# The first layer's recurrence set 6 units later in the order of work that it shares with the convolution branch's projection

## The chip, the cores and the metric

The kernel runs on one core of a Trainium2 chip. The metric is the device time in microseconds (us) of one execution; smaller is better. The engines of the core are TensorE (PE in the profile, with PEld for its weight loads), VectorE (DVE), ScalarE (ACT), GpSimd (POOL) and SyncE (SP, which issues the transfers). Each runs its own list of instructions in order and meets the others only at semaphores.

## The reference

The program is a stack of three layers over 512 tokens of width 1024 (with 256 context tokens in the first two), in fp32. What the change touches is the token mixer of the first layer. Its input projection feeds two halves: a gated linear recurrence over chunks in both directions (HGRN2), and a "chunk MLP" (the gelu branch, called the convolution branch in the change's short title; it is u and v below).

```python
def hgrn2_mixer(pl, pc, lb, onorm_w, with_ctx):
    ...
    oc_f, sc_f = gla_chunked(*fwd_c, s0)
    ol_f, _ = gla_chunked(*fwd_l, sc_f)
    oc_b, sc_b = gla_chunked(*[flip_t(a) for a in bwd_c], s0)
    ol_b, _ = gla_chunked(*[flip_t(a) for a in bwd_l], sc_b)

def chunk_mlp(u_pre, v_pre, vnorm_w, ws, bs):
    u = jax.nn.gelu(u_pre)
    v = rms_norm(jax.nn.gelu(v_pre).reshape(bsz, n, B_CHUNK, B_GROUPS, B_GROUP_DIM), vnorm_w)
    sv = jnp.einsum('gts,bnsgc->bntgc', ws, v) + bs.T[:, :, None]
    return u * sv.reshape(bsz, t_len, B_WIDTH)
```

In the recurrence each chunk of 128 tokens scores its own tokens against one another under a decay, reads the state that earlier chunks left, and updates it. A chunk therefore can't finish before the one ahead of it in its direction.

## The kernel before, in words

All that the change touches lies in one stage, `recurrence_and_mix` (L1565). Four programs share the engines in it:

- `flow`, a `Flow` (L215): the projection to v (4 tiles) and u (4 tiles) of the chunk MLP. A tile is 128 output rows by 768 tokens, summed over 8 slices, each three fp32 matmuls (high by high, high by low, low by high part), in two banks of 512 and 256 tokens (`parts=2`). On TensorE (L463) it is cut into slots of 6 matmuls, 8 to a tile. When a tile is done ScalarE runs the gelu on it (L1462; a load of the gelu table before it, and a load of the log-and-exp table behind it, L52) and then writes the high part `w_hi` of a later weight tile (L339). GpSimd then subtracts to get the low part `w_lo` (L380). VectorE multiplies u by the mixed v at the end (`gate`, L1472).
- `flow_g`: 4 more tiles of the same kind, for the recurrence's output gate (silu, L1595), right behind `flow`.
- `gl`, a `Recurrence` (L1114): 12 steps, one direction each in turn (6 chunks, 2 directions). Step n has on VectorE `keys` (L1209), `sums` (scans, L1218), `base_and_ends` (L1239, L1244), `levels` (L1228, L1229), `decayed_base` (L1256, L1257), `decayed` (L1267 to L1270), `merge` (L1289, L1292), `both` (L1300) and `update` (L1310). On ScalarE it has `log` (L1322), `grow_base` (L1330 to L1332), `grow` (L1338, L1339), `keys_back` (L1344) and `take` (L1350). On TensorE it has `turn_keys` (L1386), `scores` in two halves (L1397), `base_scores` (L1417), `read_out` (L1369, L1370) and `gain` (L1377). The stages of one step are staggered: `keys` of step n+3 stands beside `merge` of step n.
- `cm`, a `ChunkMix` (L1423): for each of the 4 tiles of v a chain between ScalarE, TensorE and VectorE: `Square` (L1486), a matmul with ones that sums (L1522), `Ln` (L1492), `Exp` (L1497), the norm (L1559), and for each of two halves a transpose (L1536), a copy (L1502), the mixing matmuls (L1544, L1547) and a copy out (L1506).

Some places hold matmuls on an identity that nothing reads (`keep_busy`, L57): 18 ahead of the first `scores`, 10 ahead of the first `turn_keys`, and 12, 6, 0 and 4 ahead of the norm of each v tile. Each fp32 matmul is two in the trace.

The four programs are generators, and `weave` (L87) takes the next piece of the program that the common list `order` names. The list is made by merging times in arbitrary units (`merged`, L81). One list serves ScalarE, VectorE and TensorE, so on each of them the instructions have one fixed order, which these times decide; the times themselves do nothing else. SyncE and GpSimd have no such list. The flows take one tile in 196/13 = 15.08 units. The recurrence's times come from `times(begin, pre, step)`: three opening slots of `pre` units, and then one slot of `step` units for each of the 12 steps, each cut in 8 turns:

```python
        order = merged(flow_times, even(flow_g.slots, flow.n * tile, (flow.n + flow_g.n + 1) * tile),
                       gl.times(0, 8, 14.3), mix_times)
```

`mix_times` hang on the flow's tiles and not on the recurrence.

Of the kernel before, what the change touches and what calls it, by code (L numbers as in the profile page):

```python
# [75 lines left out]
def even(n, a, b):  # L76

    return [a + (k + 0.5) * (b - a) / n for k in range(n)]


def merged(*times):  # L81

    turns = [(at, t) for t, own in enumerate(times) for at in own]
    return [t for _, t in sorted(turns)]


def weave(order, *programs):  # L87

    for t in order:
        next(programs[t], None)  # L90
    for program_ in programs:
        for _ in program_:
            pass
# [1471 lines left out]
def recurrence_and_mix(K, A, h_hi, h_lo, q, v, z, y_mlp, weights, x, g, nxt):  # L1565

    nc = K.nc
    with ExitStack() as c:
        W = A_HEADS * CHUNK
        rest = c.enter_context(nc.sbuf_tensor("ev_rest", [P, 17, W], F32))  # L1570
        rows = x[:, :, :].rearrange("p a t -> p (a t)").rearrange("p (r w) -> p r w", w=W)
        free = {"x": rows, "rest": rest[:, :, :]}
        at = {"x": 0, "rest": 0}

        def taken(name, n, work):
            where = "x" if name in ("k0", "k1", "S0", "S1", "kt", "ws", "gb", "sq") else "rest"
            a = at[where]
            at[where] += n
            return free[where][:, a:a + n, :]
        masks = K.rstd[:, :].rearrange("p (d t) -> p d t", d=2)  # L1580
        gl = Recurrence(K, c, q, v, z, masks, A["gla_masks"].rearrange("p (d t) -> p d t", d=2), None, taken)
        cm = ChunkMix(K, c, A["ws_t"], A["bs"], weights, y_mlp, None, taken)
        acc = [c.enter_context(nc.psum_tensor(f"uv_acc{j}", [P, 512], F32)) for j in range(3)]
        flow = Flow(K, c, "uv", A["ev_uv"], 2 * B_GROUPS, DT, h_hi, h_lo, 0, TOK,
                    [(1, cm.gelus)], [(2, cm.gate)],
                    (A["ev_g"], DT), acc=acc, parts=2, low_on_pool=True)
        space = [(cm.mixed, 2 * B_GROUPS), (cm.normed, B_GROUPS), (cm.gated, B_GROUPS - 1), (cm.gated, B_GROUPS)]

        def gates(act, f, i):
            act.wait_ge(*space[i])  # L1590
            for part in range(2):
                m = 2 * i + part
                act.wait_ge(f.mm_done, m + 1)
                at, _, width = f.banks[part]
                f.took(nc.scalar.activation(g[i][:, at:at + width], f.out(m)[:, 0:width], ACT.Silu), m)  # L1595
            K.log_and_exp()
        flow_g = Flow(K, c, "evg", A["ev_g"], A_HEADS, DT, h_hi, h_lo, 0, TOK, [(1, gates)], [], nxt, acc=acc, parts=2,
                      after=flow, then=2, low_on_pool=True)
        tile = 196 / (2 * B_GROUPS + A_HEADS + 1)
        flow_times = even(flow.slots, 0, (flow.n + 1) * tile)  # L1600
        mix_times = []
        for m in range(B_GROUPS):
            done = flow_times[(m + 1) * DT - 1]
            mix_times += even(cm.TURNS, done + 3.2, done + 3.2 + tile)
        mix_times.append(mix_times[-1] + 1)
        order = merged(flow_times, even(flow_g.slots, flow.n * tile, (flow.n + flow_g.n + 1) * tile),
                       gl.times(0, 8, 14.3), mix_times)
        with K.block() as block:
            @block.sync
            def _(sp):  # L1610
                gl.sp(sp)
                cm.sp(sp)
                weave([], flow.sp(sp))
                weave([], flow_g.sp(sp))

            @block.gpsimd
            def _(pool):
                flow.pool(pool)
                flow_g.pool(pool)

            @block.scalar
            def _(act):
                weave(order, flow.act(act), flow_g.act(act), gl.act(act), cm.act(act, flow))

            @block.vector
            def _(dve):
                weave(order, flow.dve(dve), flow_g.dve(dve), gl.dve(dve), cm.dve(dve))

            @block.tensor
            def _(pe):  # L1630
                weave(order, flow.pe(pe), flow_g.pe(pe), gl.pe(pe), cm.pe(pe))
# [2340 lines left out]
```

## Time and profile before

| | us |
|---|---|
| median of 3 runs | 2647.91 (2647.44 to 2651.93) |
| the profiled execution | 2654.73, span 2653.0 |
| TensorE busy in the span | 2522.3 (95%) |
| VectorE busy | 1669.1 (63%) |
| ScalarE busy | 988.7 (37%) |
| GpSimd busy | 172.9 (7%) |
| mean granted clock of TensorE | 0.986 |

Busy time is a sum over very different stages. The stage of this change is about a tenth of the span, from the first L463 matmul at 185.66 us to the last `update` at 438.72 us; what stands ahead of it and behind it is other code. Times in the trace are microseconds from the start of the span. TensorE's matmuls overlap, so the time that a group of them takes is best read as the distance between the starts of neighbouring groups.

### The profile page before, as it was taken

The numbers are of one execution on the slowest core, as the hardware profiler recorded it, in microseconds if no ns is written. First come the engines' busy times: TensorE is split into PE (matmuls) and PEld (weight loads), VectorE is DVE, ScalarE is ACT, GpSimd is POOL, SyncE is SP. The second block draws the span as 40 slices with busy tenths as digits, with TensorE's granted clock in tenths as the row PEclk, the third lists the DMA queues.
The fourth block names the chain that finished last, engine by engine and source line by source line (L and its number), as shares of the span: only waits on it lengthen the run. The fifth ranks groups of instructions, "written<-read, shape, count | busy, mean of one in ns | idle before, by whom it ended". The sixth has DMA issues, their size and how long they took to land. (4 is left out here: it accounts for less than half of the span.)

```text
span 2653.0 us, 36362 instructions
## 1 busy us (share of the span) xinstructions
PE 2522.3 (95%) x14741; PEld 2128.3 (80%) x14741; DVE 1669.1 (63%) x2706; ACT 988.7 (37%) x1362; POOL 172.9 (7%) x183
## 2 busy tenths in 40 slices
PE   8999899999999999999999999999989998989997
PEld 3888787788888888866679989977778886867786
DVE  5887697566767776444446756737967775354744
ACT  4235555332212222345443323325542224345532
POOL 0111011000000000012000000001610000000000
PEclk9999999999999999999999999999999999999998
DMA  6650012223343333221023443322210001211232
GB/s 261 197 160 18 23 33 88 72 87 96 101 154 119 97 104 108 70 71 48 1 72 120 137 149 125 116 82 76 80 58 17 17 9 48 96 60 68 80 103 80
DMA packets 62425, 232.26 MB, mean 88 GB/s; under 512 B 6961, under 2 KB 9649, under 8 KB 61618
## 3 DMA queue, kind: packets, MB, share of 16 engines
q1 hardware_dynamic: 46962, 173.82, 19.9%
q0 software_dynamic: 15296, 56.11, 6.7%
q8 instruction: 117, 1.92, 0.3%
q14 instruction: 50, 0.41, 0.1%
HBM read 227.02 MB, written 2.10 MB: 86 GB/s over the span
## 5 line engine op out<-in xcount | busy, mean ns | idle before, releaser
L395 DVE TENSOR_TENSOR w_lo<-w_raw,w_hi 128x1024 fp32r<-128x1024 f32 (+2 forms) x253 | 323.0, 1277 | 322.9 <-ACT w_hi L339 318.7
L339 ACT ACTIVATE w_hi<-w_raw 128x1024 fp32r<-128x1024 f32 (+4 forms) x284 | 298.1, 1050 | 253.8 <-PE late_acc L485 93.3
L485 PE MATMUL mid_acc<-mid_h_hi,w_hi 128*128 128x258 f32 x832 | 279.4, 336 | 1.5 <-DVE mid_od_fq L653 1.0
L485 PE MATMUL mid_acc<-mid_h_hi,w_lo 128*128 128x258 f32 x832 | 279.0, 335 | 0.0
L485 PE MATMUL mid_acc<-mid_h_lo,w_hi 128*128 128x258 f32 x832 | 277.1, 333 | 0.0
L485 PE MATMUL late_acc<-late_h_hi,w_hi 128*128 128x258 f32 x704 | 199.3, 283 | 0.0
L485 PE MATMUL late_acc<-late_h_hi,w_lo 128*128 128x258 f32 x704 | 198.4, 282 | 0.0
L485 PE MATMUL late_acc<-late_h_lo,w_hi 128*128 128x258 f32 x704 | 197.7, 281 | 0.0
L485 PEld LDWEIGHTS mid_acc<-mid_h_hi,w_hi 128*128 128x128 f32 x832 | 157.3, 189 | 19.4 <-issue 2.4
L485 PEld LDWEIGHTS mid_acc<-mid_h_lo,w_hi 128*128 128x128 f32 x832 | 157.5, 189 | 18.6 <-issue 1.2
L485 PEld LDWEIGHTS mid_acc<-mid_h_hi,w_lo 128*128 128x128 f32 x832 | 156.8, 189 | 16.1
L485 PE MATMUL mid_acc<-mid_y_hi,w_hi 128*128 128x256 f32 (+1 forms) x384 | 132.3, 344 | 5.8 <-DVE w_lo L395 5.2
L485 PEld LDWEIGHTS late_acc<-late_h_lo,w_hi 128*128 128x128 f32 x704 | 133.6, 190 | 0.5 <-issue 0.5
L485 PEld LDWEIGHTS late_acc<-late_h_hi,w_hi 128*128 128x128 f32 x704 | 133.1, 189 | 0.5 <-issue 0.5
L485 PEld LDWEIGHTS late_acc<-late_h_hi,w_lo 128*128 128x128 f32 x704 | 132.7, 188 | 0.0
L485 PE MATMUL mid_acc<-mid_y_lo,w_hi 128*128 128x256 f32 (+1 forms) x384 | 130.4, 340 | 0.0
L485 PE MATMUL mid_acc<-mid_y_hi,w_lo 128*128 128x256 f32 (+1 forms) x384 | 130.0, 338 | 0.0
L131 DVE CUSTOM_DVE_ANT_0 mid_scratch<-mid_side_raw,mid_rows 128x1024 f32<-128x1024 f32 x96 | 117.4, 1223 | 1.7
L3030 ACT ACTIVATE dr_low<-dr_bank 128x512 f32<-128x512 f32 x48 | 28.7, 597 | 177.5 <-PE dr_bank L3157 177.5
L485 PE MATMUL dq_acc<-s_h_hi,w_hi 128*128 128x512 f32 x200 | 85.7, 429 | 5.6 <-DVE s_h_lo L2612 4.2
L485 PE MATMUL qvz_acc<-ev_h_hi,w_hi 128*128 128x256 f32 (+1 forms) x256 | 87.1, 340 | 0.0
L485 PE MATMUL qvz_acc<-ev_h_lo,w_hi 128*128 128x256 f32 (+1 forms) x256 | 86.9, 339 | 0.0
(527 smaller groups left out, 6169.8 us busy)
## 6 DMA issues: line engine op xcount, KB each, us to landing
w_raw<-in_up SPq DMA_DIRECT2D x88, 512.0 KB, 3.6
mid_side_raw<-in_ada_t POOLq DMA_DIRECT2D x48, 512.0 KB, 3.8
w_raw<-in_down SPq DMA_DIRECT2D x32, 704.0 KB, 4.1
qvz_side_raw<-in_ada_t POOLq DMA_DIRECT2D x32, 512.0 KB, 4.3
w_raw<-in_dn_qkv SPq DMA_DIRECT2D x25, 512.0 KB, 3.2
late_side_raw<-in_ada_t POOLq DMA_DIRECT2D x24, 512.0 KB, 4.1
w_raw<-in_da SPq DMA_DIRECT2D x18, 512.0 KB, 3.2
w_raw<-in_ev_qvz SPq DMA_DIRECT2D x16, 512.0 KB, 4.3
```

Of the source, the lines that this page charges most:

```text
L131: nc.vector.tensor_tensor_reduce(out=self.scratch, in0=self.raw[:, j, :], in1=self.rows[:, m, :], scale=1.0, scalar=0.0, op0=ALU.mult, op1 ...
L339: nc.scalar.activation(K.whi[:, g % 2, 0:width], K.raw[:, g % 2, 0:width], ACT.Copy).then_inc(K.hi_done, 1)
L395: nc.vector.tensor_tensor(K.wlo[:, g % 2, 0:width], K.raw[:, g % 2, 0:width], K.whi[:, g % 2, 0:width].bitcast(F32), ALU.subtract).then_in ...
L485: last = nc.tensor.matmul(self.acc[i % len(self.acc)][:, at:at + width], left[:, j, cols], right[k][:, moving:moving + width], start=((i, ...
L3030: nc.scalar.activation(XL[G][:, :], bank[G][0][:, :], ACT.Copy).then_inc(A[G].empty, 1)
```

## The change

The recurrence's times begin at 6 units instead of 0. All of its pieces keep their order among themselves, and so do the pieces of the flows and of the chunk MLP. What changes on ScalarE, VectorE and TensorE is how the two lists are interleaved: each piece of the recurrence now stands behind the pieces of the others whose time is up to 6 units later than its old one (6/14.3 = 0.42 of a step, 6/15.08 = 0.40 of a tile). No instruction is added or removed.

```diff
         order = merged(flow_times, even(flow_g.slots, flow.n * tile, (flow.n + flow_g.n + 1) * tile),
-                       gl.times(0, 8, 14.3), mix_times)
+                       gl.times(6, 8, 14.3), mix_times)
```

Written out from the list, the order on ScalarE around the first two tiles is (numbers are the step or tile, with the half behind the point):

```
before: log0 log1 grow_base0 grow0 gelu0 w_hi square0 ln0.0 log2 ln0.1 keys_back0 exp0 grow_base1 grow1 copy0.0
        out0.0 copy0.1 take0 log3 gelu1 w_hi out0.1 square1 ln1.0
after:  log0 gelu0 w_hi square0 log1 ln0.0 ln0.1 grow_base0 grow0 exp0 log2 copy0.0 keys_back0 out0.0 copy0.1
        grow_base1 grow1 gelu1 w_hi out0.1 square1 ln1.0
```

and the end of TensorE's, with g3 as the last tile of `flow_g` (a slot each):

```
before: read_out10 g3 gain10 g3 g3 turn_keys11 scores11.0 g3 scores11.1 g3 base_scores11 read_out11 gain11
after:  read_out10 g3 gain10 g3 turn_keys11 scores11.0 scores11.1 base_scores11 read_out11 gain11
```

## Rows read from the trace of the kernel before

**Rows 1.** Stretches: width; busy (count) of PE, PEld, DVE, ACT, POOL; clock, DMA, GB/s

```profile
185.60:304.50 118.90, 106.63 (x697) 92.64 (x698) 81.71 (x182) 63.84 (x89) 12.58 (x5) 0.94 0.11 33
304.50:425.50 121.00, 115.39 (x814) 106.24 (x813) 107.10 (x255) 71.24 (x90) 16.99 (x7) 0.99 0.09 27
425.50:438.80 13.30, 10.50 (x89) 9.92 (x87) 6.00 (x16) 5.20 (x6) 2.35 (x1) 1.00 0.00 1
```

**Rows 2.** TensorE in order of time, opening: start, us, what, [idle before]

```profile
204.72 1.65 PE L1522 MATMUL cm_ps<-x,ones 128*128 128x384 f32 x2 [7.73 <-ACT x L1486]
...
211.71 4.18 PE L57 MATMUL gl_bank<-ident 128*128 128x128 f32 x36
...
223.66 2.84 PE L57 MATMUL cm_ps<-ident 128*128 128x128 f32 x24
```

**Rows 3.** TensorE in order of time, from transpose 1.1 to the sum of square 2

```profile
254.46 0.55 PE L1536 MATMUL cm_ps<-ident,x 128*128 128x128 f32 x3
254.84 1.06 PE L1377 MATMUL gl_bank<-ev_v,x 128*128 128x128 f32 x8
255.65 0.47 PE L463 MATMUL uv_acc<-ev_h_hi,w_hi 128*128 128x512 f32 x1
...
257.21 0.91 PE L1544 MATMUL cm_ps<-ev_rest,ones 1*128 1x384 f32 x2
...
258.74 0.47 PE L463 MATMUL uv_acc<-ev_h_hi,w_hi 128*128 128x512 f32 x1
...
260.20 0.60 PE L1386 MATMUL gl_bank<-ident,ev_rest 128*128 128x128 f32 x4
260.64 1.90 PE L1397 MATMUL gl_bank<-ev_rest 128*128 128x64 f32 x16
262.37 0.86 PE L1522 MATMUL cm_ps<-x,ones 128*128 128x384 f32 x2
```

**Rows 4.** ScalarE's groups, 183 to 445 us: count, busy us, mean ns, idle before

```profile
L1339 ACT ACTIVATE ev_rest<-ev_rest 128x2560 f32<-128x2560 f32 x12 | 27.9, 2327 | 0.0
...
L339 ACT ACTIVATE w_hi<-w_raw 128x1024 fp32r<-128x1024 f32 x13 | 13.8, 1059 | 3.7 <-PE uv_acc L463 2.0 <-PEq L1085 1.7
L1462 ACT ACT_TABLE_LOAD x8 | 10.3, 1283 | 0.1
...
L1462 ACT ACTIVATE x<-uv_acc 128x512 f32<-128x512 f32 (+1 forms) x16 | 7.0, 488 | 0.1
...
L1486 ACT ACTIVATE x<-x 128x768 f32<-128x768 f32 x4 | 3.3, 832 | 0.0
```

**Rows 5.** Waits, 183 to 445 us: total, times, longest

```profile
PE cm_ps L1536 <- DVE x L1559: 4.5, 2, 2.7
```

**Rows 6.** VectorE in order of time, single lines of the stage

```profile
204.37 2.84 DVE L1244 TENSOR_TENSOR ev_rest<-ev_z 128x512 f32<-128x512 f32 x1
...
304.47 0.43 DVE L1209 TENSOR_SCALAR x<-ev_z 128x512 f32<-128x512 f32 x1
...
332.38 1.98 DVE L1289 COPY_PREDICATED x<-rstd,gl_bank 128x256 f32<-128x256 uint32 x4
...
362.19 3.47 DVE L1218 TENSOR_TENSOR_SCAN ev_z<-ones,ev_z 128x128 f32<-128x128 f32 x4
...
402.06 2.12 DVE L1256 TENSOR_TENSOR ev_rest<-x,ev_rest 128x512 f32<-128x512 f32 x1
...
421.59 0.43 DVE L1267 TENSOR_TENSOR ev_rest<-ev_q,ev_rest 128x256 f32<-128x256 f32 x1 [2.73 <-ACT ev_rest L1339]
```

**Rows 7.** GpSimd in order of time, low parts of weight tiles

```profile
204.01 2.65 POOL L380 TENSOR_TENSOR w_lo<-w_raw,w_hi 128x1024 fp32r<-128x1024 f32 x1 [14.84 <-ACT w_hi L339]
...
332.43 2.40 POOL L380 TENSOR_TENSOR w_lo<-w_raw,w_hi 128x1024 fp32r<-128x1024 f32 x1 [13.57 <-ACT w_hi L339]
...
362.83 2.54 POOL L380 TENSOR_TENSOR w_lo<-w_raw,w_hi 128x1024 fp32r<-128x1024 f32 x1 [12.00 <-ACT w_hi L339]
...
401.21 2.42 POOL L380 TENSOR_TENSOR w_lo<-w_raw,w_hi 128x1024 fp32r<-128x1024 f32 x1 [14.83 <-ACT w_hi L339]
```

## What the change does to the time: a prediction

> **What bounds the kernel now.** I read the stretches of the stage first, then the waits, then each engine in order of time. The stage has three parts. In the opening, 118.9 us up to `keys6`, TensorE is busy 106.6 us and VectorE only 81.7, and the granted clock is 0.94 in the mean: about (1 - 0.94) x 118.9 = 7.1 us of clock is missing, that is some 14 us at 1.2 GHz instead of 2.4 [rows 1]. Here the four chains of the chunk MLP run between the projection's slots, and TensorE is the engine that the others wait for. From `keys6` at 304.47 us [rows 6] to the end of `decayed11` VectorE is busy 107.1 of 121.0 us and TensorE 115.4, but TensorE's matmuls overlap and its busy time flatters it [rows 1]. The steps come about every 16 us, and a step's VectorE work is about 14.5 us, to which a `gate` of 0.95 comes in four of them, so VectorE sets the beat. In the tail of 13.3 us only the last step's chain is left [rows 1].
>
> Two single facts matter. TensorE stands 7.73 us ahead of the first sum of squares, since ScalarE does `grow0`, the gelu, a `w_hi` and two table loads before the square; when it starts, the two matmuls take 1.65 us where they take 0.86 later [rows 2, 3]. And the 36 filler matmuls at 211.71 and 24 at 223.66, 4.0 and 2.7 us, cover no wait here: what they stand in front of was ready [rows 2].
>
> **Part 1, the opening: what goes.** In the new order `gelu0`, `w_hi` and `square0` stand ahead of `log1`, `grow_base0` and `grow0` on ScalarE. The gelu can start when the first tile is done at about 194.3. From there table load 1.28, `w_hi` 1.06, square 0.83 [rows 4], with 0.4 for the gelu's second half: the sum can start at about 197.9 instead of 204.7. TensorE has come to it at 196.9, so 7.7 us of waiting become 1.1, and 2.3 us of slow clock behind it go. The two waits of transposes on the norm (4.5 us together, [rows 5]) and the slow clock after the longer (about 1.7) go too, since the norm is not late there in the new order, and about 2 us of small gaps. Together 18 us go.
>
> **Part 1: what comes.** First, the norm of tile 0 now stands behind `decayed0` on VectorE, which waits for `grow0`, which waits for `ln0.1`. I walked this: sum 0.0 at 197.9, two slots, sum 0.1 to 202.2, `ln` 0.5, `grow_base0` 1.25, `grow0` 2.9 to 206.9, `decayed0` 4.0, `keys2` 0.4, norm 1.0: 212.3. TensorE has done two slots and the 24 fillers by 206.2, and waits 6.1 us; about 1.9 us of slow clock follow, by the 10 us at the low level that the 7.73 us wait brought. Second, at tiles 1, 2 and 3 ScalarE has `grow`, gelu, `w_hi`, copy out and square in a row behind the transposed half's copy: 0.5 + 2.85 + 2.2 + 2.25 + 0.5 + 0.75 = 9.05 us (2.33 of it L1339, 2 x 1.28 the tables, [rows 4]). TensorE has in that time, between transpose and next sum, a slot 1.46, mixing 1.53, a slot 1.46, and in two cases `read_out` 1.75: 4.5 to 6.2 us, so it waits 2.9 to 4.6 us each time. Before, `grow` was out of this row (6.2 us) and TensorE had 262.37 - 254.84 = 7.5 us of work in the same place, with `gain`, `turn_keys` and half the scores [rows 3], and waited for nothing. My walk gives waits of 4.9, 2.8 and 3.5 us, with 1.2 at one mixing: 12.4 us, and 1.3 of slow clock after the first. Sum of what comes: 1.1 + 6.1 + 1.9 + 12.4 + 1.3 = 22.8 us, beyond 18 less small gaps that come back (1.5): about 6 us more at equal TensorE work. Slow clock after the waits of 2.8 and 3.5 us would add up to 3; I carry 1. For the recurrence it is more, since its pieces are also 0.42 of a step later: the walk has `decayed4` end at 314.5, where it ended at 304.5. **Opening: +10.0 us** at `keys6`, with 5 and 14 as bounds (the three waits at zero for the lower, and all of them with slow clock for the upper).
>
> **Part 2, the steps in rhythm.** The same VectorE work, but two of its losses change. VectorE stood 121.0 - 107.1 = 13.9 us [rows 1], 2.73 of it at `decayed11`, behind a silu and `w_hi` that stand between `grow_base11` and `grow11` [rows 6]; in the new order they never stand there, and with VectorE busier the small waits for `gain` and `base_scores` shrink. I keep 2.9 us of idle time.
>
> Against that, the low parts on GpSimd move. Where one of them overlaps a VectorE instruction that reads two tensors from SBUF, or a scan, VectorE stands until it is over: L1244 took 2.84 us at 204.37, beside the low part at 204.01; the scans took 3.47 at 362.19 instead of 1.37, beside 362.83; L1256 took 2.12 at 402.06 instead of 0.69, beside 401.21 [rows 6, 7]. Where it overlapped four merges out of PSUM, at 332.43, they took 1.98 us, as always [rows 6, 7]. Before, the low parts of this part hit for 2.1 + 1.4 + 0.4 = 3.9 us; three of them fell on merges. In the new order a tile's last slot stands behind `base_scores` and not ahead of `turn_keys`, so gelu or silu, `w_hi` and low part come some 5 to 7 us later in the step: from 12 us after an `update`, when VectorE is in `decayed` (to 12.9), `keys`, or the next `base_and_ends` (from 14.9). Seven low parts, walked one by one: 2.1, 2.1, 2.1, 2.1, 1.2, 1.7, 1.6 = 12.9 us. So the part takes 107.1 - 3.9 + 12.9 + 2.9 = 119.0 us instead of 121.0: **-2.0 us**. With only 4 us of hits the part would be 9 us shorter than I say, at -11; with 2.1 at all seven and 8 us of idle time left it would be 125.9 us, at +5.
>
> The Trainium skill states this in the GPSIMD Engine Reference, sections Specifications and Key points: GpSimd shares its SBUF interfaces with VectorE, and they contend when a VectorE instruction has two SBUF inputs or runs in a two-port mode. It speaks against the change, and by that rule, the trace agrees: 2.84 us beside GpSimd, 0.69 alone. Taken as a full block of 2.4 us each, the seven would cost 16.8 us and not 12.9; the sum above stays with the rows.
>
> **Part 3, the tail.** The last two slots of the gate projection stood between the halves of `scores11` and ahead of `base_scores11`; now all slots are done. From the end of `decayed11`: `both10` and `update10` 1.8, `turn_keys` 0.43, scores 1.73 twice, base 0.9, last merge 0.75, `read_out` 1.8, `gain` 0.8, `update11` 1.15: 11.1 us instead of 13.3. **-2.1 us**. The slots themselves cost nothing elsewhere, since they lie in waits of TensorE for VectorE. The silu and the weight split that also stood there are done earlier or lie beside this chain. Transfers: the weight loads are released by `w_hi` and low parts and land in about 4 us, with two tiles of lead; they move by less than a tile and cost nothing.
>
> **Sum.** 10.0 - 2.0 - 2.1 = +5.9 us, and 1 for slow clock in the opening: +7 us. The profiled execution took 2654.73 us, 6.8 above the median of 2647.91; I take the shift as the same for both: 2661.7 for a profiled one, 2654.9 for the median. **2655 us.**
>
> **Rivals.**
> - *Faster: the first wait decides.* The 7.73 us and its clock are gone, and the waits at sums 1 to 3 don't arise, because `grow` ends earlier than I have it (each 2.9 us of `grow` must then be done before the transpose). The opening is then some 14 us shorter than I say, at -4, and with -2.0 and -2.1 the stage ends 8 us earlier: 2640. It decides where the three waits sum to less than about 3 us. Against it: `grow_base` and `grow` stand behind the copies in ScalarE's own order, so they can't run ahead.
> - *About the same: the low parts mostly miss.* If they fall on `both`, `update` and merges, which read PSUM, at most 4 us of the 12.9 are left: +7 - 9 = -2 us, 2646. A shift of 2 us in either engine does this, and my walk is no finer than that.
> - *Slower still.* All seven hits in full (+2), idle time of VectorE that stays at 8 us (+5): 2662.
> - That the change does nothing is out: the lists differ at nearly every entry.
>
> **How the numbers follow.** The forecast, 2650 to 2660, has 0.5; the faster rival 0.12; the low parts missing 0.22; slower still 0.16. What a measurement can tell from no change is about 0.2%, 5.3 us: below 2642.6 faster, above 2653.2 slower. Of the forecast's 0.5 I put 0.34 above that line and 0.16 within it; of the faster rival all but 0.01 below, of the missing low parts 0.02 below. Faster 0.13, same 0.37, slower 0.50. The range of 2643 to 2665 leaves out most of the faster rival and the far end of the slower one.
>
> **What would show it.** Right: TensorE's wait ahead of the first sum falls from 7.7 us to 1 or 2; a new wait of about 6 us ahead of the fillers' transpose (L1536 on the norm L1559); waits of 3 to 5 us on L1486 at the three later sums; `keys6` about 10 us later; VectorE's L1267, L1209 or L1239 with single instructions of 2 to 2.5 us; the last `update` about 11 us behind `decayed11`, where it was 13.3. Wrong: no waits on L1486 behind the first, or low parts that all lie beside merges.

## The result, and the profile after

| | before | after |
|---|---|---|
| median of five executions, us | 2650.00 (2647.44 to 2651.93) | 2673.49 (2662.23 to 2679.56) |
| ratio after / before | | 1.0073, 95% interval [1.0052, 1.0094] |
| profiled execution, us (span) | 2654.73 (2653.0) | 2662.83 (2661.1) |
| the stage, first L463 matmul to the next stage's first VectorE operation, us | 185.66 to 439.05 | to 451.57 |

The change makes the kernel slower by 0.73% (19 us; the medians lie 23.5 us apart); the forecast was 7 us, and 2673.49 lies above its range. A second series of the same kernel (`e1_again`, below) gave 1.0052 [1.0038, 1.0066], 14 us, with 11.4 us between the medians. Both are slower, and neither is 7 us. One execution of `e1_again` (5054.56 us) and one of `e3_late_split` (3629.84 us) stand far outside all others and are left out of the medians and ratios below.

The five executions of after differ more than those of before: two took 2662.2 and 2662.8 us at a mean granted clock of 0.987 and 0.986, three took 2673.5 to 2679.6 at 0.983 to 0.980. Between the first and the last lie 17.3 us; the missing clock is (1 - 0.987) x 2660.5 = 35 us in the one and (1 - 0.980) x 2677.8 = 54 us in the other, 19 us more. The missing clock is an upper bound of its cost, since clock that is missing while TensorE waits costs nothing, but it is of the size of the whole spread. The profiled execution is one of the two that lost least.

The stretches of the stage in after, divided as in [rows 1] (at `keys6`, the end of `decayed11` and the last `update`); columns are width, busy time (count) of PE, PEld, DVE, ACT and POOL, granted clock, DMA share, GB/s:

```profile
185.60:316.20 130.60, 111.80 (x715) 96.25 (x716) 76.65 (x181) 65.55 (x92) 11.85 (x5) 0.95 0.09 30
316.20:439.50 123.30, 115.25 (x807) 105.75 (x806) 116.39 (x255) 70.56 (x89) 19.18 (x7) 0.97 0.09 27
439.50:451.30 11.80, 9.12 (x78) 8.54 (x76) 5.88 (x15) 3.21 (x4) 2.36 (x1) 1.00 0.00 1
```

Against [rows 1] the opening is 11.7 us longer. TensorE is idle for 18.8 us of it, where it was for 12.3, and its busy column grows by 5.2 us, part of which is work at the low clock. The rhythm part is 2.3 us longer, with VectorE busy 116.39 us where it was 107.10. The tail is 1.5 us shorter.

TensorE in order of time in after, the instructions that had stood for over 0.8 us on ScalarE or VectorE in the opening, and one at `turn_keys5`: start, us, what, [idle before]:

```profile
197.67 0.91 PE L1522 MATMUL cm_ps<-x,ones 128*128 128x384 f32 x2 [0.83 <-ACT x L1486]
212.15 0.90 PE L1536 MATMUL cm_ps<-ident,x 128*128 128x128 f32 x3 [6.05 <-DVE x L1559]
238.88 1.65 PE L1522 MATMUL cm_ps<-x,ones 128*128 128x384 f32 x2 [4.95 <-ACT x L1486]
268.84 0.91 PE L1522 MATMUL cm_ps<-x,ones 128*128 128x384 f32 x2 [2.70 <-ACT x L1486]
293.73 0.91 PE L1522 MATMUL cm_ps<-x,ones 128*128 128x384 f32 x2 [3.09 <-ACT x L1486]
312.60 0.91 PE L1544 MATMUL cm_ps<-ev_rest,ones 1*128 1x384 f32 x2 [1.18 <-ACT x L1502]
339.27 0.70 PE L1386 MATMUL gl_bank<-ident,ev_rest 128*128 128x128 f32 x4 [3.50 <-DVE ev_rest L1310]
```

The 7.73 us wait of [rows 2] is gone and a row of new ones stands behind it. The second and the third take 0.90 and 1.65 us for what takes 0.55 in [rows 3] and 0.91 in the rows below: they run at 1.2 GHz. The clock around the two long waits in after (columns as above):

```profile
203.20:210.00 6.80, 2.90 (x26) 2.71 (x25) 4.57 (x11) 4.13 (x5) 0.00 (x0) 1.00 0.00 0
210.00:216.80 6.80, 4.65 (x22) 4.66 (x23) 6.76 (x17) 1.12 (x2) 0.00 (x0) 0.50 0.00 0
...
237.40:244.20 6.80, 5.32 (x20) 4.62 (x21) 0.24 (x1) 2.01 (x4) 2.35 (x1) 0.50 0.25 77
```

The clock halves (0.50 of 2.4 GHz) from 210.0 and from 237.4, each time within the wait and on for 4.6 and 5.3 us of the work behind it. VectorE's instructions from `keys6` on that took far longer than others of their line (x4: four scans together):

```profile
319.68 2.79 DVE L1239 TENSOR_TENSOR ev_rest<-ev_z 128x512 f32<-128x512 f32 x1
...
334.84 2.47 DVE L1209 TENSOR_SCALAR x<-ev_z 128x512 f32<-128x512 f32 x1
...
355.58 2.50 DVE L1209 TENSOR_SCALAR x<-ev_z 128x512 f32<-128x512 f32 x1
...
369.94 2.57 DVE L1267 TENSOR_TENSOR ev_rest<-x,ev_rest 128x256 f32<-128x256 f32 x1
...
395.64 3.52 DVE L1218 TENSOR_TENSOR_SCAN ev_z<-ones,ev_z 128x128 f32<-128x128 f32 x4
...
412.80 3.50 DVE L1218 TENSOR_TENSOR_SCAN ev_z<-ones,ev_z 128x128 f32<-128x128 f32 x4
...
425.59 1.98 DVE L1239 TENSOR_TENSOR ev_rest<-ev_z 128x512 f32<-128x512 f32 x1
```

and beside them GpSimd's low parts:

```profile
319.54 2.39 POOL L380 TENSOR_TENSOR w_lo<-w_raw,w_hi 128x1024 fp32r<-128x1024 f32 x1 [24.54 <-ACT w_hi L339]
333.29 3.74 POOL L380 TENSOR_TENSOR w_lo<-w_raw,w_hi 128x1024 fp32r<-128x1024 f32 x1 [11.36 <-ACT w_hi L339]
354.73 3.07 POOL L380 TENSOR_TENSOR w_lo<-w_raw,w_hi 128x1024 fp32r<-128x1024 f32 x1 [17.70 <-ACT w_hi L339]
369.79 2.45 POOL L380 TENSOR_TENSOR w_lo<-w_raw,w_hi 128x1024 fp32r<-128x1024 f32 x1 [11.98 <-ACT w_hi L339]
396.11 2.46 POOL L380 TENSOR_TENSOR w_lo<-w_raw,w_hi 128x1024 fp32r<-128x1024 f32 x1 [23.87 <-ACT w_hi L339]
412.67 2.72 POOL L380 TENSOR_TENSOR w_lo<-w_raw,w_hi 128x1024 fp32r<-128x1024 f32 x1 [14.11 <-ACT w_hi L339]
424.67 2.35 POOL L380 TENSOR_TENSOR w_lo<-w_raw,w_hi 128x1024 fp32r<-128x1024 f32 x1 [9.28 <-ACT w_hi L339]
```

All seven that fall in the part stop VectorE. Less the usual 0.69, 0.43, 0.43, 0.42, 1.37, 1.37 and 0.69 us of the same work, the seven take 13.9 us too much. The Trainium skill says in the GPSIMD Engine Reference, section Key points, that GpSimd's SBUF interfaces are VectorE's too, for instructions with two SBUF inputs or in a two-port mode; the trace agrees for those with two inputs. L1209 reads a single tensor and stood all the same; by that page it would be of the second kind, but no run here shows in which mode it runs.

The first two stops have a sequel: they make the `update` behind them late, `turn_keys5` waits for that (3.50 us above), the clock halves from 339.8 to 346.6, the scores are late, and VectorE stands in its turn:

```profile
348.08 0.90 DVE L1289 COPY_PREDICATED x<-rstd,gl_bank 128x256 f32<-128x256 uint32 x2 [2.88 <-PE gl_bank L1397]
```

In `e17_after_cut` below, the same order with these low parts cut short, that wait of `turn_keys5` (L1388 there) falls to 0.15 us:

```profile
338.17 0.66 PE L1388 MATMUL gl_bank<-ident,ev_rest 128*128 128x128 f32 x4 [0.15 <-DVE ev_rest L1312]
```

### The profile page after: what moved, and what is told of

Same layout as the page of the kernel before. It is cut to its first block and busy times, and to the rows that moved or that the text cites. A ratio compares the mean times of both kernels' runs of the same rounds, so it can differ in the third digit from the quotient of the medians.

```text
span 2661.1 us, 36361 instructions
## 1 busy us (share of the span) xinstructions
PE 2521.9 (95%) x14741; PEld 2127.7 (80%) x14741; DVE 1673.1 (63%) x2706; ACT 987.7 (37%) x1361; POOL 174.4 (7%) x183
```

## The experiments

The questions. Theory A, from the prediction and the trace of after: the loss has three parts, the new order itself (waits at full clock), the clock that halves in the waits, and VectorE beside GpSimd. Rivals: the loss is the opening alone; or the steps alone; or something behind the stage. The experiments divide the change in place (`e4`, `e5`, `e6`), move the low parts (`e3`, `e7`), hold the clock by filling waits (`e2`, `e12`, `e13`) and take the low parts away (`e9`, `e10`, `e14` to `e18`). Each ratio is to the kernel before, run in the same series on the same chip. Diffs are against the kernel after, unless said otherwise.

**The change again**, with nothing edited.

> The changed kernel once more, to see where the executions differ from the profiled one. The profiled execution took 2662.8 us, 12.9 us over the median of the kernel before, which is what a walk through the orders gives for this stage (+10 in the opening, -2, -2); but three of five executions took 2673.5 to 2679.6 us with a mean granted clock of 0.980 to 0.983 instead of 0.986. Theory A (clock): the new short waits of TensorE in the opening (6.05, 4.95, 3.09, 2.70 us) are followed by the low clock in some executions and not in others. Then the longer executions are longer inside the stage from 185 to 451 us, by low clock that the trace shows there. Theory B (elsewhere): the stage takes 265 us in all executions, and the rest of the kernel runs at a lower clock in some. The median is expected at 2668 to 2678 by both; if a trace of a longer execution comes, the place of the low clock tells them apart.

Median 2665.76 against 2654.33: 1.0052 [1.0038, 1.0066]; its executions lie between 2662.5 and 2674.3 us, and their mean is 13.7 us above that of before. Its profiled execution took 2674.32 us, and its stage ends at 459.1, 7.5 us behind that of the other profile. It is the same kernel, with the same waits (6.04, 4.95, 2.72 and 3.09 us in the opening); what differs is the clock. Its stretches at 1.2 GHz up to 356 us (columns as above):

```profile
211.80:218.60 6.80, 5.94 (x28) 5.94 (x29) 5.97 (x15) 1.03 (x2) 0.00 (x0) 0.50 0.00 0
...
239.10:245.90 6.80, 5.88 (x21) 5.09 (x22) 0.00 (x0) 1.44 (x3) 2.17 (x1) 0.50 0.27 77
269.90:273.30 3.40, 3.02 (x6) 2.12 (x7) 0.00 (x0) 0.91 (x2) 1.64 (x1) 0.50 0.25 33
297.20:300.60 3.40, 3.40 (x13) 2.86 (x12) 1.20 (x5) 1.10 (x2) 0.64 (x1) 0.50 0.49 142
345.00:355.20 10.20, 10.20 (x44) 9.62 (x43) 5.50 (x16) 5.90 (x8) 0.00 (x0) 0.50 0.00 0
```

Here all four long waits halve the clock, where in the first profile two did. The stage spends 34 us at 1.2 GHz, against 20.5 in the first profile of after and 17.1 in before.

**The waits filled.** Filler matmuls go where the four long waits of the opening were, so that TensorE works through them. Another 12 were meant for the wait at `turn_keys5`.

> The changed kernel with matmuls on the identity, which nothing reads, put into TensorE's waits: 34 instead of 12 ahead of the norm of tile 0 (wait of 6.05 us), 18, 9 and 10 ahead of the sums of squares 1, 2 and 3 (4.95, 2.70, 3.09 us), 12 ahead of turn_keys 5 (3.50 us). The waits themselves stay, so nothing but the granted clock can change. Theory A (clock decides the spread and some 11 us of the median): no fall of the clock in the stage, the spread of the executions shrinks to 5 us, and the median comes to 2654 to 2660 (the profiled 2662.8 less 3 to 8 us of low clock). Theory B (the clock falls elsewhere): median and spread stay within 3 us of the changed kernel's. Theory C (the order alone costs what the median shows): the clock in the stage is 1.0 and the median stays at 2670 or more.

```diff
-    BUSY_KEYS = {0: 10}
+    BUSY_KEYS = {0: 10, 5: 12}
...
+                    if g:
+                        pe.wait_ge(self.gl.merged, 5 * g)
+                        K.keep_busy(self.gl.ps_s[0][:, 0:P], (0, 18, 9, 10)[g])   # ahead of sum g
...
-                    K.keep_busy(self.ps[:, 0:P], (12, 6, 0, 4)[g])
+                    K.keep_busy(self.ps[:, 0:P], (34, 6, 0, 4)[g])                # ahead of the transpose
```

Median 2662.16, 1.0032 [1.0021, 1.0043], executions 2657.9 to 2666.0. The waits in the opening shrink to 1.13, 0.94, 0.71 and 0.88 us, `keys6` starts at 311.3 (316.2 and 320.7 without), and 4 us between the medians, 5.5 between the means, are gone. No work of the kernel was moved, and the wait for a merge that the edit adds shows no idle time in the trace, so these were clock. They are less than filling the opening is worth, because the fillers of `turn_keys5` missed their wait: in `turn_keys` the wait for the `update` stands ahead of `keep_busy`, so they came behind it and were work more, some 4.3 us up to L1386:

```profile
334.36 4.44 PE L57 MATMUL gl_bank<-ident 128*128 128x128 f32 x24 [3.49 <-DVE ev_rest L1310]
338.63 0.60 PE L1386 MATMUL gl_bank<-ident,ev_rest 128*128 128x128 f32 x4
```

Against the first profile of after, `keys6` is 4.9 us earlier and the stage ends (450.9) only 0.7 us earlier. `e12`, `e13`, `e14` and `e11` below have such fillers too (4.4, 2.6, 1.9 and 2.1 us in their traces); `e15` and `e18` don't. The opening of `e2` and the rest of the stage (columns as above):

```profile
185.60:311.30 125.70, 120.02 (x833) 105.22 (x832) 76.62 (x181) 65.28 (x92) 11.81 (x5) 1.00 0.10 31
311.30:450.60 139.30, 128.59 (x906) 118.49 (x904) 122.39 (x269) 73.73 (x92) 21.52 (x8) 0.96 0.08 24
```

**Only the short waits filled**: as above, but none at the transpose (12 as in the kernel) nor at sum 1.

> The changed kernel with fillers in its shorter waits only: 9 and 10 ahead of the sums of squares 2 and 3 (2.7 and 3.1 us) and 12 ahead of turn_keys 5 (3.5 us); the waits of 6.05 us ahead of the norm's transpose and 4.95 us ahead of the first sum stay bare. The clock fell behind the two long waits in every trace of this kernel, but behind the sums 2 and 3 only in the longer execution. Theory A says that the short ones make the spread and the gap between the profiled execution and the median: then executions within 5 us of one another, median 2660 to 2665 with low clock only behind the two long waits. If the long ones decide: 2666 or more.

Median 2668.87, 1.0065 [1.0051, 1.0079]: nothing gained at the end. Its clock halves at 209.8 and 237.1, in the waits of 6.05 and 5.00 us, and no longer in the short ones; `keys6` comes at 316.1, as in the first profile of after and 4.6 us ahead of `e1_again`. Behind that it has the 4.4 us of misplaced fillers. So the run shows that the two long waits bring the slow clock by themselves, but not that the short ones cost nothing.

**Low parts later in the step.** The split of a weight tile is issued at a later turn.

> The changed kernel with the high part of each weight tile of both projections (ScalarE), and with it the low part (GpSimd), four turns later in the tile, so that the low parts fall beside the merges again and no longer beside VectorE's instructions with two SBUF inputs. Theory D (the seven or so hits of 1.2 to 2.1 us are paid by the end, about 13 us in all against 4 before): VectorE has no instruction of over 2 us in the steps in rhythm, and the time is 6 to 10 us below that of the changed kernel. Theory E (TensorE bounds the steps as well, VectorE's stalls are hidden): the long instructions vanish and the time falls by less than 3 us. In the opening the square no longer stands behind the high part (2.25 us less in front of each sum), which by the walk takes up to 2 us from each of the waits at sums 1 to 3: 3 to 6 us more.

```diff
-                    (A["ev_g"], DT), acc=acc, parts=2, low_on_pool=True)
+                    (A["ev_g"], DT), acc=acc, parts=2, low_on_pool=True, split_turn=5)
...
-                      after=flow, then=2, low_on_pool=True)
+                      after=flow, then=2, low_on_pool=True, split_turn=5)
```

Median 2662.84, 1.0032 [1.0020, 1.0044]. Three to five us better than `e1_again`, but this didn't take the stalls away: behind `keys6` they moved to scans (323.5, 340.9, 358.3) and to L1257 and L1256 (364.9, 428.5), and four came into the opening, where the one at 207.7 goes with a wait on the norm of 8.19 us instead of 6.05. `e7_late_split7`, the same with 7 in place of 5:

> The changed kernel with the high and low parts six turns later in the tile instead of four, since with four they fell on the scans just ahead of the merges (VectorE's long instructions were still worth 10 us in the steps in rhythm, of 14). With six they should fall on the merges, which read PSUM. Theory D (the stalls of VectorE beside GpSimd are paid by the end): at most two instructions of over 2 us in the steps in rhythm, the stretch from keys 6 to the last update takes 125 to 128 us instead of 135, and the time is 8 to 12 us below that of the changed kernel. Theory E (they are hidden): the stretch stays at 131 or more.

Median 2666.04, 1.0054 [1.0042, 1.0067]. Behind `keys6` low parts again hit a scan (319.7) and L1256, L1257 and L1267 (341.3 to 428.9). Neither run isolates the stalls. With VectorE busy nine tenths of the time, a low part of 2.4 us finds nearly no place.

**The change by halves.** Only the three opening slots of the recurrence's times are later, and closer together, so that its steps begin at 24 units as before (`e4`); or only the steps are 6 units later (`e5`); or all is 3 units later in place of 6 (`e6`).

> The recurrence begins at 6 units, but its three opening slots are 6 units wide instead of 8: 6 + 3 x 6 = 24, so its twelve steps stand where they stand in the kernel before, and only the start is late. Theory F (the first wait of 7.7 us is won, the losses come from the steps' place): 4 to 8 us faster than the kernel before, no waits on the later squares, low parts beside the merges as before. Theory G (the late start itself costs: the norm of tile 0 waits for decayed of step 0): the first wait is gone but one of 3 to 6 us ahead of the norm's transpose stands in its place, and the time is within 4 us of the kernel before.

```diff
-                       gl.times(6, 8, 14.3), mix_times)
+                       gl.times(6, 6, 14.3), mix_times)
```

> The complement of the last experiment's opening: the recurrence's three opening slots stand where they stand in the kernel before (0 to 24 units), and only its twelve steps are 6 units later, as in the changed kernel. Theory F (the losses come from the steps' place, the opening's shift is a gain of about 9 us): TensorE's first wait is 7.7 us again, the waits on the squares 1 to 3 (5, 3, 3 us) and the low parts beside VectorE's own work are there, and the time is 20 to 30 us above the kernel before, that is 8 to 12 us above the changed kernel. Theory G (the late opening is what costs in the changed kernel): the time is within 5 us of the kernel before.

```diff
-                       gl.times(6, 8, 14.3), mix_times)
+                       [t if t < 24 else t + 6 for t in gl.times(0, 8, 14.3)], mix_times)
```

> Half the change: the recurrence begins at 3 units instead of 6. Its first grow_base and grow then stand at 19.5 and 20.5 units, still behind the first gelu (17.9) and square (18.0), so the first wait of 7.7 us goes here as well; grow of steps 1, 2 and 3 stands at 29.7, 44.0 and 58.3 units, ahead of the second halves' copies at 30.5, 45.6 and 60.7 and 3 to 5 units ahead of the gelus. Theory H (what costs is grow directly ahead of gelu, high part and square on ScalarE): no waits of over 2 us at the squares 1 to 3, and the time is 3 to 10 us below the kernel before. Theory I (the cost grows with the shift): it is between the two, at 5 to 9 us above the kernel before.

```diff
-                       gl.times(6, 8, 14.3), mix_times)
+                       gl.times(3, 8, 14.3), mix_times)
```

| kernel | median, us (before beside it) | ratio | `keys6` | end of the stage |
|---|---|---|---|---|
| `e4_opening_only` | 2645.01 (2654.33) | 0.9963 [0.9950, 0.9975] | 295.2 | 429.8 |
| `e5_steps_only` | 2671.68 (2652.64) | 1.0075 [1.0061, 1.0088] | 321.1 | 460.0 |
| `e6_begin3` | 2651.97 (2652.64) | 0.9997 [0.9988, 1.0006] | 297.1 | 436.7 |
| before, profiled | | | 304.5 | 439.05 |

The change is the sum of two opposite ones. Its opening slots alone, with the gelu of tile 0 ahead of `grow0`, are worth 9 us: the first wait falls to 1.10 us, the one on the norm of tile 0 doesn't come up, and the opening runs at full clock throughout (columns as above):

```profile
185.60:295.20 109.60, 103.04 (x697) 89.33 (x698) 81.83 (x181) 62.43 (x88) 12.32 (x5) 1.00 0.11 36
```

The steps alone cost 19 us, and have waits of 7.23, 5.84, 2.71 and 3.12 us with 44 us at 1.2 GHz. The sum of the two, 10 us, is near the change's 11 to 14 in the second series. `e4` beats both kernels. With 3 units the three waits at the sums aren't there: the point at which `grow` comes into ScalarE's row ahead of the square lies between 3 and 6. In `e6` the wait of an L463 on a gelu is 5.04 us (at 356.61; 1.75 in before), and the low parts hit scans; its total is that of before.

**Fewer fillers.** In `e4` the fillers stand in front of work that is ready, as in [rows 2]. `e8_opening_trim` leaves most of them out, `e11_trim_held` puts 9 at `turn_keys5` besides (`BUSY_KEYS = {0: 0, 5: 9}`). Against `e4`:

> The order that was 9 us faster than the kernel before (opening at 6 with slots of 6 units), with fewer matmuls that nothing reads: none instead of 10 ahead of the first turn_keys, 10 instead of 18 ahead of the first scores, 6 instead of 12 ahead of the norm of tile 0. In that kernel's trace they stood in front of work that was ready, and a wait of 2.3 us for decayed of step 0 is left to cover. Expected by those rows: 4 to 5.5 us below the opening alone, about 2640. If the granted clock falls in the opening for want of them, the gain is lost: 2645 or more, with low clock between 200 and 230 us.

```diff
-    BUSY_KEYS = {0: 10}
+    BUSY_KEYS = {0: 0}
...
-                self.K.keep_busy(self.ps_s[0][:, 0:P], 18)
+                self.K.keep_busy(self.ps_s[0][:, 0:P], 10)
...
-                    K.keep_busy(self.ps[:, 0:P], (12, 6, 0, 4)[g])
+                    K.keep_busy(self.ps[:, 0:P], (6, 6, 0, 4)[g])
```

> The shifted opening with trimmed fillers, whose opening was 3 us shorter than without the trimming (keys 6 at 292.1 us instead of 295.2) but whose last update ended at the same time: its trace shows 10.2 us at the low clock from 315.5 us, behind a wait of 2.31 us ahead of turn_keys 5, where the untrimmed one has 3.4 us. This kernel has 9 matmuls on the identity (2.0 us) in that wait. Theory A (short waits are paid through the clock): no low clock between 310 and 340 us, the last update some 3 us earlier (at about 426.5 instead of 429.5), the time 2640 to 2643. Rival: the steps in rhythm are bound by VectorE and absorb the 3 us whatever the clock: last update at 429.5 and 2644 to 2646.

Medians 2644.68, 0.9972 [0.9961, 0.9983], and 2645.15, 0.9973 [0.9962, 0.9983]: no better than `e4`. In `e8` `keys6` comes 3.1 us earlier than in `e4`, and the stage ends at the same 429.8, with 10.2 us at 1.2 GHz from 315.5 (3.4 us in `e4`); in `e11` the low stretch is at 217.1 (6.8 us) instead, and `keys6` is back at 295.3. The expectation of `e11` failed. It didn't test what it was meant to, since its 9 fillers came behind the wait at `turn_keys5` (2.33 us). Why the clock falls at 217.1, where TensorE was busy throughout, stays open; the wait ahead of that, 1.69 us, is in `e8` as well (1.68), and there the clock stays up.

**Without the low parts.** To price the stalls, GpSimd computes 128 of the 1024 columns of each low part, so seven eighths of the low parts are left out of the computation.

```diff
-            nc.gpsimd.tensor_tensor(K.wlo[:, g % 2, 0:width], K.raw[:, g % 2, 0:width],
-                                    K.whi[:, g % 2, 0:width].bitcast(F32), ALU.subtract).then_inc(K.lo_done, 1)
+            nc.gpsimd.tensor_tensor(K.wlo[:, g % 2, 0:P], K.raw[:, g % 2, 0:P],
+                                    K.whi[:, g % 2, 0:P].bitcast(F32), ALU.subtract).then_inc(K.lo_done, 1)
```

The order of before with this is `e9_before_short_low`, with its waits filled too `e14_before_filled_short_low`; the order of after is `e10_after_short_low` and, with the fillers of `e2` in the opening alone, `e15_after_filled_short_low`. `e13_before_filled` is before with its waits filled alone (30 ahead of the first sum, 10 and 10 at the norms; `BUSY_KEYS = {0: 10, 5: 8}`, which again comes behind its wait).

> The kernel before with GpSimd's low parts in this stage cut to the first 128 of each row's 1024 columns (the other seven eighths of the low part are left out, so the projection's result lacks that correction): each takes about 0.35 us instead of 2.4 and can stall VectorE for no more than that. It is the partner of the next run. Before, VectorE's long instructions beside GpSimd are worth about 10 us in the whole stage (2.1 us at 204, 238, 261 and 362, 1.4 at 402, 0.4 at 386), most of them where TensorE or ScalarE is what the stage waits for. Theory D (stalls are paid by the end): 3 to 5 us below the kernel before. Theory E (hidden): within 2 us of it.

> The changed kernel with the same cut of the low parts. In its trace the stalls are worth 14 us in the steps in rhythm alone. Theory D: it is 10 to 16 us faster than the changed kernel (2668), so 3 us below to 5 above the kernel before, and the stretch from keys 6 to the last update takes 122 to 126 us instead of 135. Theory E: it is less than 5 us faster than the changed kernel.

> The kernel before with fillers in its own waits: 30 ahead of the first sum of squares (7.7 us), 10 instead of 0 and 4 ahead of the norms' transposes of tiles 2 and 3 (2.7 and 1.7 us), 8 ahead of turn_keys 5 (2.3 us). Partner of the changed kernel with its waits filled (2662, 6 us below the unfilled). Its low clock in the opening is 13.7 us, of which some 8 lie beside work. Theory J (each order loses by the clock, the changed one some 6 us and the old one about 4): 2647 to 2650. Theory K (only the changed order loses by the clock): 2651 or more.

> The kernel before with both taken away, VectorE's stalls beside GpSimd (low parts cut to an eighth) and the bare waits (filled). By the single runs: stalls -9.1, clock -2 to -5 if theory J holds; the sum is 2638 to 2641. It is the baseline of the next run: what is left between the two is the order alone, by waits of one engine for another.

> The changed kernel with both taken away: its stalls were worth 17 us (2668 to 2651) and its bare waits 6 (2668 to 2662). If the two are independent: 2645, with keys 6 at 312 us and 127 us from there to the end of the stage. Then the order alone is worth 4 to 6 us beside the partner run, stalls 8 and clock 2 to 4 of the 15 us that the change costs. If filling no longer helps once the stalls are gone (2650 or more), the clock mattered only through them.

This cut also reached three projections of the second layer whose low parts GpSimd computes, so only differences between these kernels hold, not their distance to before. The last three restrict it to the flows of this stage (`if self.name in ("uv", "evg"): width = P` ahead of the same line).

> The kernel before, with GpSimd's low parts of this stage's flows alone computed on 128 of 1024 columns (seven eighths of these low parts are left out; the second layer's keep their whole width). Theory A (about 8 to 9 us of the change's price is VectorE and GpSimd standing beside each other, 8.0 us of such stalls in the old order with its waits filled): the stage's own share here is 2 to 5 us below before, about 2648 to 2650, and the second layer's share of the earlier cut was 5 to 7 us. Rival B (the second layer had no share): 2643 again.

> The changed kernel with the same cut of this stage's low parts alone. Theory A: 10 to 12 us below the changed kernel, 2656 to 2658, which is 6 to 8 us above the kernel before with the same cut. Rival B: 2651 again.

> The changed kernel with its four long waits filled (as in e2_filled) and this stage's low parts cut. Theory A (order alone +2 to 3, clock 5 to 6, stalls about 9): 2650 to 2653, that is 4 to 7 us below e17_after_cut and 1 to 4 us above e16_before_cut. Rival B (the sizes came from the second layer's low parts): no nearer to e16_before_cut than e2_filled is to the kernel before, 8 us above it.

Medians as distance to the kernel before of the same series, us, with the ratio:

| | low parts whole | cut everywhere | cut in the stage alone |
|---|---|---|---|
| order of before | 0 | `e9` -9.1, 0.9965 [0.9952, 0.9977] | `e16` -1.8, 0.9993 [0.9984, 1.0002] |
| the same, filled | `e13` -1.0, 0.9995 [0.9986, 1.0003] | `e14` -9.0, 0.9961 [0.9948, 0.9973] | |
| order of after | `e1` +11.4 (+13.7 by the means), `e12` +16.6 | `e10` -1.2, 0.9997 [0.9988, 1.0005] | `e17` +6.6, 1.0026 [1.0017, 1.0035] |
| the same, filled | `e2` +7.8 | `e15` -6.8, 0.9970 [0.9958, 0.9982] | `e18` -0.3, 0.9997 [0.9988, 1.0006] |

An interval is 2 to 4 us wide to each side, so single entries are no finer than that; what carries is that the differences repeat. The second layer's share of the cut is 6.5 to 7.8 us in all three pairs where both columns are filled, whatever the order, so it drops out. Then:

- **Clock, new order.** Filling the waits takes 6.9 us from `e17` (to `e18`) and 5.6 from `e10` (to `e15`). From `e1` to `e2` it takes 3.6, or 5.5 by the means, with the misplaced fillers against it.
- **Clock, old order.** Filling takes 1.0 us, or nothing (`e9` to `e14`), again with misplaced fillers, 1.9 to 2.6 us of them. So what the old order loses by its clock lies between nothing and some 3.6 us (1.0 + 2.6) and stays open. In `e13` `keys6` is 4.5 us earlier than in before.
- **VectorE beside GpSimd.** In the order of after the stage's low parts cost 4.8 us (`e1` to `e17`; 6.9 by the means) and 8.1 (`e2` to `e18`, of which up to 4.3 are the misplaced fillers of `e2`), in that of before 1.8. With their sequel through the clock, which is in these numbers, that is net 3 to 6 us, the upper number a bound; by the pairs that are cut everywhere and filled it is (7.8 + 6.8) - (-1.0 + 9.0) = 6.6, with the same reserve.
- **The order alone**, filled and cut: `e15` - `e14` = 2.2 us, less than the two intervals, or up to 4.1 without the misplaced fillers of `e14`.

The parts overlap and can't be added up more finely than this; measured directly, the change costs 11.4 (`e1`), 16.6 (`e12`) and 23.5 us in the first series. No sum of them reaches the 23.5: that series has five executions spread over 17 us, and why three of them were long isn't shown. The rivals are out: the opening's slots alone gain (`e4`), the steps alone cost more than the whole change (`e5`), and what lies behind the stage takes 2213.4 us in the profile of `e1_again` and 2214.0 in that of before.

The opening and the rest of the stage in `e17` and, behind them, in `e18` show the clock's part by itself, the same work but for the fillers, and no long VectorE instruction in either:

```profile
185.60:316.80 131.20, 112.38 (x706) 96.51 (x707) 75.67 (x181) 65.15 (x92) 2.27 (x5) 0.93 0.10 30
316.80:443.90 127.10, 121.75 (x892) 113.06 (x891) 109.34 (x269) 73.82 (x93) 12.16 (x8) 1.00 0.09 26
```

```profile
185.60:310.80 125.20, 119.54 (x831) 104.83 (x830) 75.30 (x181) 64.82 (x92) 2.28 (x5) 1.00 0.10 31
310.80:436.30 125.50, 120.12 (x882) 111.42 (x880) 109.46 (x269) 73.41 (x93) 12.17 (x8) 1.00 0.09 26
```

6.0 us of the 7.6 between their ends lie in the opening, where the clock is 0.93 in one and 1.00 in the other: missing are 0.07 x 131.2 = 9 us of clock, part of it in the waits themselves, where it costs nothing. And VectorE's busy time tells the stalls without a count by hand: over the stage it is 194.8 us in before and 198.9 in after, 185.5 in `e16` and 185.0 in `e17`. So the low parts cost VectorE 9.3 us in the old order, of which 1.8 reached the end, and 13.9 in the new one, of which 5 to 8 did. In the old order 5.5 of the 9.3 us lay in the opening (81.7 busy in [rows 1], 76.2 in `e16`), where VectorE has room; in the new one 1.0 does (76.65 against 75.67), and 12.9 lie behind `keys6`.

## Why the prediction was wrong

**The mechanism was right in the waits and the stops.** The waits of TensorE in the opening were foreseen as 1.1, 6.1, 4.9, 2.8, 3.5 and 1.2 us and came as 0.83, 6.05, 4.95, 2.70, 3.09 and 1.18. `keys6` was foreseen 10 us later; it was 11.7 later in one profile and 16.2 in the other. The seven hits on VectorE were put at 12.9 us and took 13.9. The tail was to shrink to 11.1 us and took 11.8.

**The step that failed is the slow clock.** In the opening the prediction let 2.3 + 1.7 us go with the old waits and 1.9 + 1.3 + 1 come with the new, +0.2 in all, and for the steps in rhythm it put the clock at nothing. What was to come was too small: measured, the new order's waits in the opening cost 5.6 and 6.9 us by their clock (`e15`, `e18`), not 4.2, though either number has some 3 us of noise. It was priced as if each wait did once what it did in the trace before. In after, two of four waits halve the clock in one execution and all four in another, and in both the wait at `turn_keys5` does so as well, with 20.5 and 34 us at 1.2 GHz in the stage, of which 6.8 and 13.6 lie behind `keys6`; at half the clock that is 3.4 and 6.8 us of work, where the prediction had nothing. What was to go, 4.0 us, is neither shown nor refuted: `e13` won 1.0 us, but it carried 2.6 us of fillers behind a wait.

**With it failed the idle time of VectorE in the steps.** The prediction kept 2.9 of 13.9 us. It was 6.9 us in the first profile of after and 10.1 in `e1_again` (126.4 us from `keys6` to the end of `decayed11`, VectorE busy 116.35), while the busy time came as foreseen (116.4 us; 107.1 - 3.9 + 12.9 = 116.1). So the part that was to lose 2.0 us took 2.3 and 5.4 more. Part of this is the clock again: 2.88 us are the wait of the merge at 348.08, the sequel of two stops by GpSimd and of the clock behind them. The prediction had added the stops up as VectorE's own and followed none of them into TensorE's queue. The rest is the order itself. With the low parts cut in both orders, the time from `keys6` to the stage's end falls from 133.8 us (`e9`) to 127.1 (`e10`), 6.7 us, where the prediction had 11.0 of idle time and 2.1 of tail. Without clock and stops it had the new order 2.2 us faster (7 - 9.0 - 0.2); it is 2.2 us slower, or more, by medians whose intervals overlap (`e15` and `e14`).

**Last, the line that carries the shift from the profiled execution over to the median.** For a profiled one the prediction said 2661.7, and 2662.83 was measured, but that was luck: the stage was 12.5 us longer, not 7, and what lies behind the stage was 4.5 us shorter in that execution (2209.5 us where before has 2214.0; 2213.4 in `e1_again`). The median of after lies above its profiled execution in the first series and below it in the second, while the profiled execution of before had stood 6.8 us above the median that the forecast started from. With a term whose size changes from one execution to the next, one profiled execution doesn't stand for the median. The first series fell on the long side: three of its five executions took over 2673 us, one of five in the second.

**The stops: right in size on the engine, too large at the end.** Behind `keys6` they are 12.9 us by the busy columns, where before has 107.1 + 6.0 - 109.3 = 3.8 ([rows 1], and the second stretch of `e16`, which holds the tail as well). That is 9.1 us more, and 9.0 were foreseen; 3 to 6.6 of them reached the end. VectorE was taken to set the beat for the whole of the part. That some of the stops fell where another engine was as late would explain the rest, but no run shows which.

**The rivals.** "The first wait decides" is wrong as put, but `e4` shows that its mechanism is real: where only the opening slots move, 9 us are gained. "The low parts mostly miss" and "all in full" are both wrong; the idle time of the latter, 8 us, stood at 123.3 - 116.4 = 6.9 us in one profile and at 10.1 in the other. None of the rivals had the clock as its mechanism, and this is what a range reaching to 2665 lacked; `keys6` in `e1_again`, 16.2 us later, lies beyond the upper bound of 14.

## What to carry to other kernels

A change of order is read as a list of waits that go and waits that come, and those can be worked out from an engine's rows to half a us. What a wait of 3 to 6 us then costs on TensorE isn't only its length: add the slow clock behind it for every such wait and take the case that all of them bring it, since executions differ in this. A stop of another engine is followed into the waits behind it, and not only added up on its own engine. When fillers are to price a wait, look for the wait in front of the filler in the trace: if it is still there, the fillers stand behind it and the run measures something else. If a shift helps at the start of a stage and hurts in its rhythm, try each half alone; here one half is worth -9 us and the other +19.

## What was not expected of the hardware

- Waits of 2.7 and 3.1 us leave the clock up in one execution of after and halve it in another (`e1_again`); the two longer ones halved it in both, and in `e12`.
- Taking out fillers that cover no wait won 3.1 us at `keys6` in `e8` and nothing at the end; the clock was then low at 315.5 for 10.2 us, where `e4` has 3.4 us, and in `e11` at 217.1.
- GpSimd pays as well when it meets VectorE: two of the low parts above took 3.74 and 3.07 us instead of 2.35 to 2.4. And a VectorE instruction that reads a single tensor, L1209, stood like those that read two: 2.47 and 2.50 us instead of 0.43. Merges out of PSUM (L1289) kept their 1.9 us in after, as in [rows 6].
- A cut of GpSimd's low parts in three projections of the second layer is worth 6.5 to 7.8 us by itself. Which instructions wait there wasn't looked into.
